# Expert layer: order of the first gate chunks, products whose results are not read, the last expert's bank, and the order of the final norm

## The reference

```
h = rms_norm(x, g_ffn) * (1 + sc2) + sh2
aff = softmax(h @ w_router)                       # 256 tokens x 16 experts
gate, idx = top_k(aff.T, 32)                      # each expert chooses 32 tokens
xe = h[idx]                                       # 16 x 32 x 1024
hid = silu(xe @ w_gate) * (xe @ w_up)             # 16 experts, 1024 x 1024 each
ye = (hid @ w_down) * gate
x = x + gt2 * scatter_add(ye)                     # back to the 256 tokens
out = rms_norm(x, g_final)
```

## Time and profile before

| | us |
|---|---|
| median of 3 runs | 1873.3 |
| lowest and highest | 1872.92, 1877.81 |
| the profiled execution | 1879.08 |
| its span, first to last instruction | 1877.3 |
| TensorE busy in the span | 1623.2 (86%) |
| DVE, ACT, POOL busy | 864.5, 662.0, 135.6 |
| mean granted clock of TensorE | 0.907 |
| read from memory | 413.91 MB |

### The profile page before, as it was taken

One profiled execution on the slowest core, in us unless ns is written; L12 is line 12 of the kernel. 1 busy time (PEld: TensorE's weight loads), 2 busy tenths in 40 slices (PEclk: granted clock), 3 DMA queues, 4 the chain that ended last, 5 costly groups with the idle time before them and its releaser, 6 DMA issues.

```text
span 1877.3 us, 35170 instructions
## 1 busy us (share of the span) xinstructions
PE 1623.2 (86%) x14772; PEld 1326.3 (71%) x14772; DVE 864.5 (46%) x1224; ACT 662.0 (35%) x866; POOL 135.6 (7%) x184
## 2 busy tenths in 40 slices
PE   7999999999979999998999998898868676666575
PEld 7999799979959789987888797697865222222222
DVE  5855466546555356654557676944650000000001
ACT  5444355435344345434444643524432000000000
POOL 6700000000000000000005002030110000000000
PEclk9999999999999999999999998998988777686776
DMA  7755556755627556645342242102677999999996
GB/s 231 264 185 182 178 165 193 267 204 177 205 68 247 183 167 185 191 162 165 97 151 91 90 158 77 38 25 68 231 296 317 421 421 420 421 421 421 421 421 259
DMA packets 249789, 417.04 MB, mean 222 GB/s; under 512 B 12926, under 2 KB 210993, under 8 KB 225073
## 3 DMA queue, kind: packets, MB, share of 16 engines
q1 hardware_dynamic: 248481, 411.82, 61.2%
q10 hardware_dynamic: 1168, 3.17, 0.5%
HBM read 413.91 MB, written 1.05 MB: 221 GB/s over the span
## 4 chain that ended last, share of the span: by engine, by line
issue 34%; PE 32%; DMA 23%; DVE 4%; POOL 3%; ACT 3%; SPq 0%; DVEq 0%; ACTq 0%; POOLq 0%
DMA w_exp<-in_w_down_dram 10%; DMA w_exp<-in_w_gate_dram 6%; DMA w_exp<-in_w_up_dram 6%; PE bank L409 3%; PE bank L410 3%; PE bank L411 3%; PE bank L1705 3%; PE bank L2423 1%; PE bank L1008 1%; PE bank L1007 1%; PE bank L1006 1%; PE bank L426 1%; PE bank L427 1%; PE bank L428 1%; POOL ang L843 1%
## 5 line engine op out<-in xcount | busy, mean ns | idle before, releaser
L248 DVE TENSOR_TENSOR w_lo<-w_raw,w_hi 128x2048 fp32r<-128x2048 f32 (+2 forms) x178 | 400.3, 2251 | 287.0 <-ACT w_hi L241 286.8
L241 ACT ACTIVATE w_hi<-w_raw 128x2048 fp32r<-128x2048 f32 (+2 forms) x178 | 334.1, 1880 | 152.6 <-DMA w_raw<-in_ffn_w_down_dram 57.5
L409 PE MATMUL bank<-h_hi,w_hi 128*128 128x256 f32 x1248 | 353.2, 283 | 5.5 <-DVE h_lo L610 3.9
L410 PE MATMUL bank<-h_lo,w_hi 128*128 128x256 f32 x1248 | 351.0, 281 | 0.0
L411 PE MATMUL bank<-h_hi,w_lo 128*128 128x256 f32 x1248 | 350.9, 281 | 0.0
L2423 PE MATMUL bank<-w_exp,xeT 128*32 128x256 f32 x2048 | 176.0, 483 | 88.8 <-DMA w_exp<-in_w_up_dram 53.8
L409 PEld LDWEIGHTS bank<-h_hi,w_hi 128*128 128x128 f32 x1248 | 240.2, 192 | 10.5 <-issue 6.8
L410 PEld LDWEIGHTS bank<-h_lo,w_hi 128*128 128x128 f32 x1248 | 238.7, 191 | 0.0
L411 PEld LDWEIGHTS bank<-h_hi,w_lo 128*128 128x128 f32 x1248 | 238.4, 191 | 0.0
L2423 PEld LDWEIGHTS bank<-w_exp,xeT 128*32 128x32 f32 x2048 | 66.3, 130 | 193.1 <-DMA w_exp<-in_w_up_dram 91.9
L2423 PE MATMUL bank<-w_exp,hT 128*32 128x256 f32 x1024 | 102.8, 543 | 50.7 <-DMA w_exp<-in_w_down_dram 49.2
(11 more groups left out here) (504 smaller groups left out, 2990.1 us busy)
## 6 DMA issues: line engine op xcount, KB each, us to landing
w_exp<-in_w_gate_dram SPq DMA_DIRECT2D x64, 1024.0 KB, 26.9
w_exp<-in_w_up_dram SPq DMA_DIRECT2D x64, 1024.0 KB, 26.9
w_exp<-in_w_down_dram SPq DMA_DIRECT2D x64, 1024.0 KB, 26.9
w_raw<-in_ffn_w_gu_dram SPq DMA_DIRECT2D x88, 512.0 KB, 5.0
w_raw<-in_w_in_dram SPq DMA_DIRECT2D x54, 512.0 KB, 4.6
w_mod<-in_w_mod_dram SPq DMA_DIRECT2D x24, 1024.0 KB, 7.8
w_raw<-in_ffn_w_down_dram SPq DMA_DIRECT2D x44, 512.0 KB, 4.2
w_raw<-in_mem_w_kv_dram SPq DMA_DIRECT2D x32, 512.0 KB, 4.7
```

Source lines behind the costliest of these rows:

```text
L241: e.activation(whi[slot][:, 0:w], raw[slot][:, 0:w], ACT.Copy).then_inc(S["hi_ready"], 1)
L248: e.tensor_tensor(wlo[slot][:, 0:w], raw[slot][:, 0:w], whi[slot][:, 0:w].bitcast(F32), ALU.subtract).then_inc(S["lo_ready"], 1)
L409: e.matmul(dst, whi[slot][:, lo:hi_], bh[:, k, :], start=(k == 0), stop=False)
L410: e.matmul(dst, whi[slot][:, lo:hi_], bl[:, k, :], start=False, stop=False)
```

## The change

- The first expert's gate chunk j is multiplied in the gather: chunk 0 after feature 2, 1 after feature 4, 2 after feature 6, 3 after feature 7 (`first_gate`). Each waits for the eviction of its second feature. The wait for `SG` moves from the start of the experts to `turn_gates`.
- Products of `warm` (three copies of the identity in fp32r, made by one ACT instruction) with itself, 128x384 each, whose results nothing reads: 5 behind the router, 17 behind the transposes of the softmax, 3 behind those of the positions, all into `G[3]`; 4 behind each of the eight gate and up chunks of the last expert, into `XG[0]`; 2, 5 and 6 behind its down chunks 1, 2 and 3, into `XT`.
- The down chunks of the last expert go into `XG[0]` in place of `XD`, without the wait for `y` of the expert before.
- `group_out` goes through the column halves first and the token halves second. For the last group the first half waits only for two of the four instructions of `y`.
- In the final norm DVE multiplies three of the four banks by the gain vector as soon as each has been squared. When a token half has its factor, ACT scales its first column half and DVE its second; only the fourth bank is still multiplied by factor and gain in one instruction. A store waits for both parts.

```diff
@@ -176,7 +176,8 @@
             for t_ in range(TT):
-                e.wait_ge(*rows_done[t_])
+                for w in rows_done[t_]:
+                    e.wait_ge(*w)
                 e.dma_start(out[0][t_ * P:(t_ + 1) * P, :], x[:, t_, :]).then_inc(stored, 16)
@@ -2282,6 +2283,25 @@
+    warm = place("warm", [P, 384], F32R, offset=sbuf_at["rope1"])
+    t_warm = act.do(lambda e: e.activation(warm[:, :].rearrange("p (a j) -> p a j", a=3),
+                                           ident[:, :].rearrange("p (a j) -> p a j", a=1).broadcast_to((P, 3, P)), ACT.Copy), *t_o)
+    def unread(e, bk, n):
+        for _ in range(n):
+            e.matmul(bk[:, 0:384], warm[:, 0:P], warm[:, :], start=True, stop=True)
+    def unread_in_G(n, *free):
+        waits = [t_warm, *free, *bank_free[3]]
+        def run(e):
+            for w in waits:
+                e.wait_ge(*w)
+            unread(e, G[3], n)
+        pe.raw(run)
     def router_part(c):
@@ -2303,6 +2323,7 @@
     t_log = router_part(3)
+    unread_in_G(5)
     rs, rq = small[:, 136:138], small[:, 138:140]
@@ -2345,6 +2366,7 @@
         tp = pe.do(lambda e, t_=t_: e.transpose(X[1][0:E, t_ * P:(t_ + 1) * P], a0[:, t_, :], ident[:, :]), t_aff, xfree[1])
+    unread_in_G(17)
     t = dve.do(lambda e: e.tensor_copy(cur[:, 0, :], X[1][0:E, 0:SEQ]), tp, *cap_free)
@@ -2358,6 +2380,7 @@
         tp = pe.do(lambda e, t_=t_: e.transpose(X[0][:, t_ * E:(t_ + 1) * E], ps[:, t_ * P:(t_ + 1) * P], ident[0:E, 0:E]), t, xfree[0])
+    unread_in_G(3)
     t = dve.do(lambda e: e.tensor_copy(a1, X[0][:, 0:TT * E].rearrange("p (t n) -> p t n", t=TT)), tp)
@@ -2371,7 +2394,33 @@
+    e_used, e_silu, e_hid, e_turned, e_hT, e_yev, e_gates, e_out = (nc.alloc_semaphore(n_) for n_ in (
+        "expert_chunk_used", "expert_silu", "expert_hidden", "expert_turned", "expert_hidden_T",
+        "expert_y_dve", "gates_turned", "expert_group_out"))
+    XG, XD, XT = X[0:2], X[2], X[3]
+    chunk_at = {key: n_ for n_, key in enumerate(order())}
+    W4 = D // 4
+    def expert_chunk(e, name, x_, j, dst, lhs):
+        n_ = chunk_at[name, x_, j]
+        e.wait_ge(e_in[n_ % NSLOT], 16 * (n_ // NSLOT + 1))
+        for kk in range(2):
+            for c in range(4):
+                ins = e.matmul(dst[32 * c:32 * c + 32, :], lhs(2 * j + kk),
+                               wexp[n_ % NSLOT][:, kk, c * W4:(c + 1) * W4],
+                               start=(j == 0 and kk == 0), stop=(j == 3 and kk == 1))
+        ins.then_inc(e_used, 1)
     xe_at = {}
+    def first_gate(j):
+        def run(e):
+            e.wait_ge(*xe_at[2 * j + 1])
+            expert_chunk(e, "w_gate_2", 0, j, XG[0][:, 0:W4], lambda k: xeT[:, k, 0:C])
+        pe.raw(run)
     for k in range(KT):
@@ -2381,15 +2430,12 @@
         bank_free[b] = [xe_at[k]]
+        if k in (2, 4, 6):
+            first_gate(k // 2 - 1)
+    first_gate(3)
     done_before = [(S["pe_done"], pe.n), (S["act_done"], act.n), (S["dve_done"], dve.n), act_evacs(), dve_evacs()]
...
     NCH = 12 * E
-    e_used, e_silu, e_hid, e_turned, e_hT, e_yev, e_gates, e_out = (nc.alloc_semaphore(n_) for n_ in (
-        "expert_chunk_used", "expert_silu", "expert_hidden", "expert_turned", "expert_hidden_T",
-        "expert_y_dve", "gates_turned", "expert_group_out"))
-    XG, XD, XT = X[0:2], X[2], X[3]
-
-    chunk_at = {key: n_ for n_, key in enumerate(order())}
@@ -2407,39 +2453,32 @@
-    W4 = D // 4
-
     def pe_experts(e):
-        e.wait_ge(*t_SG)
-
-        def chunk(name, x_, j, dst, lhs):
-
-            n_ = chunk_at[name, x_, j]
-            if n_ < 4:
-                e.wait_ge(*xe_at[2 * j + 1])
-            e.wait_ge(e_in[n_ % NSLOT], 16 * (n_ // NSLOT + 1))
-            for kk in range(2):
-                for c in range(4):
-                    ins = e.matmul(dst[32 * c:32 * c + 32, :], lhs(2 * j + kk),
-                                   wexp[n_ % NSLOT][:, kk, c * W4:(c + 1) * W4],
-                                   start=(j == 0 and kk == 0), stop=(j == 3 and kk == 1))
-            ins.then_inc(e_used, 1)
-
         def gate_up(x_):
...
                 for j in range(4):
-                    chunk(name, x_, j, XG[x_ % 2][:, o_:o_ + W4], lambda k: xeT[:, k, x_ * C:(x_ + 1) * C])
+                    if x_ == 0 and o_ == 0:
+                        continue
+                    expert_chunk(e, name, x_, j, XG[x_ % 2][:, o_:o_ + W4], lambda k: xeT[:, k, x_ * C:(x_ + 1) * C])
+                    if x_ == E - 1:
+                        unread(e, XG[E % 2], 4)
...
             e.wait_ge(e_hT, x_ + 1)
-            if x_:
+            if x_ == E - 1:
+                into = XG[E % 2]
+            elif x_:
                 e.wait_ge(e_yev, x_)
+                into = XD
             else:
                 e.wait_ge(e_gates, 2)
+                into = XD
             for j in range(4):
-                chunk("w_down_2", x_, j, XD[:, 0:W4], lambda k: hT[x_ % 2][:, k % 2, (k // 2) * C:(k // 2 + 1) * C])
+                expert_chunk(e, "w_down_2", x_, j, into[:, 0:W4], lambda k: hT[x_ % 2][:, k % 2, (k // 2) * C:(k // 2 + 1) * C])
+                if x_ == E - 1:
+                    unread(e, XT, (0, 2, 5, 6)[j])
@@ -2454,6 +2493,7 @@
+            e.wait_ge(*t_SG)
             for g_ in range(E // 4):
@@ -2468,9 +2508,9 @@
-            e.wait_ge(e_yev, 4 * g_ + 4)
-            for t_ in range(TT):
-                for hf in range(2):
+            for hf in range(2):
+                e.wait_ge(e_yev, 4 * g_ + 4 + (hf if g_ == E // 4 - 1 else 0))
+                for t_ in range(TT):
                     e.matmul(G[2 * t_ + hf][:, :], GT[:, g_, t_ * P:(t_ + 1) * P], ye[:, g_, hf * BANK:(hf + 1) * BANK],
@@ -2536,10 +2576,12 @@
             e.wait_ge(*used("w_down_2", x_, 3))
+            from_ = XG[E % 2] if x_ == E - 1 else XD
             for c in range(4):
                 ins = e.tensor_tensor(ye[32 * (x_ % 4):32 * (x_ % 4) + 32, x_ // 4, c * W4:(c + 1) * W4],
-                                      XD[32 * c:32 * c + 32, 0:W4], gt[32 * c:32 * c + 32, 1, c * W4:(c + 1) * W4], ALU.mult)
-            ins.then_inc(e_yev, 1)
+                                      from_[32 * c:32 * c + 32, 0:W4], gt[32 * c:32 * c + 32, 1, c * W4:(c + 1) * W4], ALU.mult)
+                if c == 3 or (c == 1 and x_ == E - 1):
+                    ins.then_inc(e_yev, 1)
@@ -2551,25 +2593,26 @@
     msq, rstd = small[:, 128:132], small[:, 136:138]
-    rows_done = []
-    for t_ in range(TT):
-        for hf in range(2):
-            cs = slice(hf * BANK, (hf + 1) * BANK)
-            t = act.do(lambda e, t_=t_, hf=hf, cs=cs: e.activation(
-                xn[:, t_, cs], G[2 * t_ + hf][:, :], ACT.Square, scale=D ** -0.5, accum_out=msq[:, 2 * t_ + hf:2 * t_ + hf + 1]),
-                (e_out, outs - 4 + 2 * t_ + hf + 1))
-        t = dve.do(lambda e, t_=t_: e.scalar_tensor_tensor(
-            out=rstd[:, t_:t_ + 1], in0=msq[:, 2 * t_:2 * t_ + 1], scalar=EPS, in1=msq[:, 2 * t_ + 1:2 * t_ + 2],
-            op0=ALU.add, op1=ALU.add), t)
-        t = pool.do(lambda e, t_=t_: e.tensor_tensor(rstd[:, t_:t_ + 1], rstd[:, t_:t_ + 1], neg_half[:, 0:1], ALU.pow), t, t_nh)
-        rows_done.append(t)
-    for t_ in range(TT):
-        for hf in range(2):
-            cs = slice(hf * BANK, (hf + 1) * BANK)
-            t = dve.do(lambda e, t_=t_, hf=hf, cs=cs: e.scalar_tensor_tensor(
-                out=x[:, t_, cs], in0=G[2 * t_ + hf][:, :], scalar=rstd[:, t_:t_ + 1], in1=gf2[:, cs],
-                op0=ALU.mult, op1=ALU.mult), rows_done[t_], (g2_in, 16))
-        rows_done[t_] = t
+    inv_rms, gained_rows, squared = {}, {}, {}
+    for n_, (hf, t_) in enumerate((hf, t_) for hf in range(2) for t_ in range(TT)):
+        cs = slice(hf * BANK, (hf + 1) * BANK)
+        summed = (e_out, outs - 4 + n_ + 1)
+        squared[t_] = act.do(lambda e, t_=t_, hf=hf, cs=cs: e.activation(
+            xn[:, t_, cs], G[2 * t_ + hf][:, :], ACT.Square, scale=D ** -0.5, accum_out=msq[:, 2 * t_ + hf:2 * t_ + hf + 1]), summed)
+        if hf:
+            t = dve.do(lambda e, t_=t_: e.scalar_tensor_tensor(
+                out=rstd[:, t_:t_ + 1], in0=msq[:, 2 * t_:2 * t_ + 1], scalar=EPS, in1=msq[:, 2 * t_ + 1:2 * t_ + 2],
+                op0=ALU.add, op1=ALU.add), squared[t_])
+            inv_rms[t_] = pool.do(lambda e, t_=t_: e.tensor_tensor(rstd[:, t_:t_ + 1], rstd[:, t_:t_ + 1], neg_half[:, 0:1], ALU.pow), t, t_nh)
+        if n_ < 3:
+            gained_rows[t_, hf] = dve.do(lambda e, t_=t_, hf=hf, cs=cs: e.tensor_tensor(
+                x[:, t_, cs], G[2 * t_ + hf][:, :], gf2[:, cs], ALU.mult), squared[t_], (g2_in, 16))
+    c1 = slice(BANK, 2 * BANK)
+    rows_done = [[act.do(lambda e, t_=t_: e.activation(x[:, t_, 0:BANK], x[:, t_, 0:BANK], ACT.Copy, scale=rstd[:, t_:t_ + 1]),
+                         inv_rms[t_], gained_rows[t_, 0])] for t_ in range(TT)]
```

(3 more changed lines are left out.)

## The result

| us | before | changed |
|---|---|---|
| median of 5 runs each | 1875.69 | 1857.02 |
| lowest and highest | 1872.92 to 1879.06 | 1853.98 to 1864.66 |
| the profiled execution | 1879.08 | 1864.66 |
| its span | 1877.3 | 1862.9 |

The ratio on record is 0.9897, 95% interval 0.9867 to 0.9928: faster, though by less than 2%, and by 18.7 us between the medians, where 9.4 was forecast. (The ratios on record are not quotients of medians, and differ from them a little: here the quotient is 0.9900.) Measured again beside the first experiments (12 runs of the changed kernel, 35 of the one before) the ratio is 0.9940, interval 0.9918 to 0.9962, medians 1864.11 and 1875.39: 11.3 us. Both intervals lie under 1, and the forecast's 9.4 to 10.4 lies in the second interval, not in the first.

A forecast was written before the change was run, and what follows sets the result against it. The DMA queues reading the experts' weights at 421 GB/s were taken as the bound, only the stretch's ends movable. Front 5.4 plus back 5.0 made 10.4 us, less 1.0: 1873.3 - 9.4 = 1863.9 us, range 1859.5 to 1869.5.

The forecast's parts named there:

- The front's order: First expert's gate chunks between the gather's features: weights flow earlier, a lead of 3.3 us at half clock throughout.
- The front's clock: Router and gather: unread products from 1400.73 bring full clock before the gather at 1407.97; 2.1 us of the sum.
- The lead: Weight stream behind the gather: chunks 18 to 20 flow early, so the stream runs 5.4 us ahead of before.
- The end: Behind the last chunk: halves, clock and final factor together save 5.0 us; the store's 3.1 us stays.
- the halves: Last expert's output products start when half of `ye` is done, 1863.2 instead of 1864.04: 0.85 us.
- the output products: Last expert's four output products at full clock, 0.85 us each in place of 1.7: 3.1 us more.
- the final factor: Final norm: one product instead of four behind the sum, from last square to last product 2.3 instead of 3.64: 1.05 us.
- the clock is not held: Rival for both ends: TensorE falls back to half clock, gain 5.0 us, time 1868.3; chance 0.11.
- The lead wasn't lost: Denies the rival that lone transfers, gain vector or a longer stream end eat the front's lead: 1868.3; chance 0.09.
- the lone transfers: Chunks 18 to 20, each alone on the queues: 4.4 us each, paid one behind the other, would leave 1.7 lead.
- priced like fp32: Rival "Slower": unread products in router and last expert go at fp32's rate, 1875.4 to 1879; chance 0.06.
- from the sum to the median: Last step: 1.0 us off the sum for its dependence on the clock, 9.4 off the median of 1873.3: 1863.9.

The follow-up runs named there:

- the first experiments: First group of switched variants of the changed kernel, on another chip, both kernels measured again beside them: ratio changed to before 0.9940, medians 1864.11 and 1875.39 us.
- e1_no_gates: Changed kernel with the first expert's four gate chunks behind the whole gather again; ratio 0.9960 to the kernel before, median 1868.64 us.
- e2_pairs_more: Changed kernel with the first expert's gate and up chunks multiplied in pairs in the gather and 22 unread products instead of 17; ratio 0.9944 to the kernel before.

## Why the prediction was right and where it failed

**Right: what bounds the kernel and where the time can go.** The queues' stretch stayed at 421 GB/s and its two ends moved. The time from the gather's start to the end fell by 9.5 us (two traces of each kernel); the sum was 10.4. That they come so close is in part luck: 1.1 of the 9.5 is the late landing, which the sum doesn't have, and the front's own part fell short by more than the total shows.

**The front's order: right.** 3.3 us at half clock; 2.9 measured alone, and 3.0 between e1_no_gates and the changed kernel.

**The front's clock: failed.** "With products since 1400.73 I expect it up before 1407.97" came true in all eight traces, but the sum needs more, that it stays up, and that held in one. In the changed kernel's first trace the clock rose under the products, but seventeen of them were done at 1400.35, 1.6 us before the transposes, and it fell again at 1402.3. I had sized the row for products at half clock, which would just have filled the gap, and did not follow what happens when they speed up in the middle. Chunk 0 started at 4.1 to 4.7 behind the gather instead of 3.0. The lead was 5.3 and 3.7 instead of 5.4; without the 1.1 us of the late landing it was 4.2 and 2.6.

**The end: right.** 0.77 for the halves (0.85), 2.9 for the output products (3.1 with what the late rise gave), 0.93 for the final factor (1.05): 4.6 of 5.0. The rival "the clock is not held" was true of the front and false of the back. By the Trainium skill, TensorE: Matmul & The Clock Gate, Loop structure matters more than you think, long waits for transfers between matmuls cost the clock. The traces agree in four of the five without the 45 products (13.09 us from the last chunk to the end, and 16.2 to 17.1), and with products in the waits the output products kept the clock in nine of nine.

**The rivals.** The lead wasn't lost, and the lone transfers did not pay one behind the other: in the changed kernel's first trace chunks 18 and 19 each landed 4.7 us behind their issue, but 3.05 us apart, as they were issued. The 2.0 us of fixed time that the prediction took from the Trainium skill, DMA: Bandwidth & Descriptors, Anatomy of one DMA, are given there for transfers that GpSimd issues; these are SP's. The unread products are not priced like fp32: 22 of them took 5.30 us in the first trace of e2_pairs_more, part of it at half clock, and nothing behind them was late.

**Failed: from the sum to the median.** The step is "I take 1.0 off for this: 1873.3 - 9.4 = 1863.9", with the range 1859.5 to 1869.5 around it. I saw that three runs spread by 4.9 us and used it only to shave the gain. The range was built from the unknown prices of the change alone and left out what is larger: the same kernel's median was 1857.02 over five runs and 1864.11 over the next twelve, and its single runs went from 1853.98 to 1872.15, while 35 runs of the kernel before went from 1866.07 to 1885.03.

Leaving out the spread is the step that failed; it does not explain the whole distance. The twelve later runs have a standard deviation of 3.9 us, and among them no draw of five has a median as low as 1857.02, since four of the first five lie below the fastest of the twelve. So something besides chance between runs may have differed on that first occasion, whose chip isn't on record and when the kernel before measured as it did later (1875.69 and 1875.39). Of the 18.7 us some 10 are the change's, by the traces and by the later times. Traces of equal code show that the shared front varies by up to 19 us, but not that it gave the other 7 to 9: only one of the five runs has a trace, and their cause stays open. Their mean granted clocks were 0.920 to 0.926, against 0.915 to 0.923 in the twelve; no run tests whether that is cause or company.

The forecast of 1863.9 is within 0.3 us of the later median, and this too is luck in part: the baseline was 2.1 us too low (1873.3, later 1875.39) and the gain 1.9 too small (9.4, later 11.3), and the two cancel.

## What to carry to other kernels

Compare two profiled executions from a common event just ahead of the change, not from the span's start: here that took the scatter from 19 us to under 2 us and gave each part its price in one or two traces. Put the run-to-run spread of the shared work into the range of a forecast, not only the prices of the edit, and measure on a second occasion before explaining a gain that is twice the sum. When unread products are to hold TensorE's clock over a gap, size them for the speed that they will reach, since they halve the time that they cover once they succeed.

## What the runs showed of the hardware

The granted clock can fall while products are being issued in bursts: at 1402.3, 1.9 us behind the last of 17 products, with the positions' transposes and the first of three more products already issued; TensorE had been idle for 1.6 us at a time and no longer. One stage of back-to-back products at granted clock 1.00 took 118.7 us in four traces and 114.4 in ten, and nothing between, in code that all share. The stream of weights does not end sharply: the last five microseconds run at about half rate (217 GB/s before, 183 behind), in every trace. And within it one transfer of 1 MB in some 62 lands 3.2 to 4.1 us behind the one before in place of 2.49.
